# Counts of the experts held in registers, TensorE's branches in another order, and earlier signals in a mixture-of-experts layer

## The reference

```
logits = t @ w_router + b_router
top_val, top_idx = top_k(logits, 2);  gates = softmax(top_val)
for each expert e, with the tokens that chose it:
    y_e = (silu(x_e @ w_gate_e[e]) * (x_e @ w_up_e[e])) @ w_down_e[e]     # 1024 -> 3584 -> 1024
y = sum over a token's two experts of gate * y_e
```

## Time and profile before

| | |
|---|---|
| median of 3 runs | 1678.16 us (1676.92 to 1680.18) |
| the profiled execution | 1674.14 us, of which the span of its instructions is 1672.3 us |
| granted clock of TensorE, mean | 0.952 |
| TensorE busy | 1478.1 us, 88% of the span |
| DVE, ACT busy | 781.4 us, 589.6 us |
| read and written | 488.89 MB, 292 GB/s on average |

### The profile page before, as it was taken

One profiled execution on the slowest core, in us unless ns is written; L12 is line 12 of the kernel. 1 busy time (PEld: TensorE's weight loads), 2 busy tenths in 40 slices (PEclk: granted clock), 3 DMA queues, 4 the chain that ended last, 5 costly groups with the idle time before them and its releaser, 6 DMA issues.

```text
span 1672.3 us, 30627 instructions
## 1 busy us (share of the span) xinstructions
PE 1478.1 (88%) x12402; PEld 1185.7 (71%) x12403; DVE 781.4 (47%) x1097; ACT 589.6 (35%) x793; POOL 69.4 (4%) x66
## 2 busy tenths in 40 slices
PE   5999899999999998756579999999996679999894
PEld 3878778999977886644458875588985468888452
DVE  2584565565546655100028851177761036665112
ACT  2445253444344432100027740156551025554101
POOL 0010100000010111000000000000000000000002
PEclk8999999999999999987789999999998789999998
DMA  9644467745433528899999999997567996555893
GB/s 362 236 161 175 192 229 291 287 170 196 158 100 123 227 76 362 350 424 424 424 424 426 426 410 426 424 406 285 236 281 306 424 424 245 225 226 227 328 426 151
DMA packets 69183, 488.89 MB, mean 292 GB/s; under 512 B 7744, under 2 KB 7776, under 8 KB 11168
## 3 DMA queue, kind: packets, MB, share of 16 engines
q1 hardware_dynamic: 66800, 479.94, 71.0%
q10 hardware_dynamic: 1648, 4.59, 0.8%
q0 software_dynamic: 576, 2.10, 0.4%
HBM read 482.66 MB, written 3.93 MB: 291 GB/s over the span
## 4 chain that ended last, share of the span: by engine, by line
PE 44%; DMA 9%; issue 4%; DVE 2%; SPq 1%; ACT 1%; POOL 1%; ACTq 0%; POOLq 0%; DVEq 0%
PE PG L1443 9%; DMA ring<-in_experts 6%; PE PG L1500 4%; PE Y L1528 4%; PE Y L1455 4%; PE TRB L1500 4%; PE PG L1565 4%; DMA arena<-in_experts 3%; PE TRB L1506 3%; PE PG L1506 3%; PE Y L1613 2%; PE Y L1519 2%; PE TRB L1429 2%; SPq L786 1%; PE Y L1252 1%
## 5 line engine op out<-in xcount | busy, mean ns | idle before, releaser
L2570 DVE COPY arena<-TRB 128x64 f32<-128x64 f32 (+1 forms) x70 | 17.6, 251 | 343.0 <-PE TRB L1429 343.0
L1443 PE MATMUL PG<-ring,mixT 128*32 128x128 f32 (+1 forms) x1920 | 117.4, 352 | 65.2 <-issue 60.6
L1677 ACT ACTIVATE rope<-PG 64x128 f32<-64x128 f32 (+2 forms) x84 | 27.2, 324 | 378.7 <-PE PG L1443 356.2
L1443 PEld LDWEIGHTS PG<-ring,mixT 128*32 128x32 f32 (+1 forms) x1920 | 90.6, 139 | 95.9 <-issue 81.4
L1677 ACT ACTIVATE parts<-ring 128x2048 fp32r<-128x2048 f32 x81 | 151.8, 1901 | 9.1 <-DMA ring<-in_weights 4.0
L945 PE MATMUL PG<-h_parts,parts 128*128 128x512 f32 x432 | 152.9, 394 | 1.4 <-DVE arena L2448 1.4
L1443 PE MATMUL PG<-arena,mixT 128*32 128x128 f32 (+1 forms) x1664 | 102.2, 353 | 42.0 <-issue 42.0
L1443 PEld LDWEIGHTS PG<-arena,mixT 128*32 128x32 f32 (+1 forms) x1664 | 79.2, 140 | 69.4 <-issue 56.3
L947 PE MATMUL PG<-h_parts,parts 128*128 128x256 f32 x432 | 121.9, 282 | 0.0
L2433 DVE TENSOR_TENSOR parts<-ring,parts 128x2048 fp32r<-128x2048 f32 x42 | 95.1, 2289 | 30.4 <-ACT parts L1677 30.4
L2554 DVE TENSOR_TENSOR parts<-arena,parts 128x2048 fp32r<-128x2048 f32 x42 | 95.2, 2287 | 17.0 <-PE Y L1519 14.4
(11 more groups left out here) (384 smaller groups left out, 2839.8 us busy)
## 6 DMA issues: line engine op xcount, KB each, us to landing
ring<-in_experts SPq DMA_DIRECT2D x168, 1024.0 KB, 17.1
arena<-in_experts SPq DMA_DIRECT2D x168, 1024.0 KB, 18.9
ring<-in_weights SPq DMA_DIRECT2D x116, 1024.0 KB, 6.4
ring<-in_weights SPq DMA_DIRECT2D x4, 512.0 KB, 5.1
ypairs<-hT ACTq DMA_DIRECT2D x3, 512.0 KB, 7.0
tok<-in_x SPq DMA_DIRECT2D x1, 1024.0 KB, 9.0
result<-scr SPq DMA_DIRECT2D x2, 512.0 KB, 2.6
ring<-in_weights SPq DMA_DIRECT2D x2, 432.0 KB, 6.2
```

What stands on the lines that cost most here:

```text
L1443: last = mm(bank[i * n:(i + 1) * n, 0:width], xe[:, k, 0:n], w[k // 4][:, k % 4, i * width:(i + 1) * width], start=(k == 0), stop=(k == KD ...
L1677: return nc.scalar.activation(out_, in_, func, **kw)
```

## The change

- **Counts.** Each engine loads all eight counts into eight registers ahead of the loop, and shifts them down by one register (seven moves) with each expert. `pick` is gone.
- **Branches.** On TensorE `first_variant` is 32: its tests are 256, 192, 160, 128, 64, and the 32-row body comes right behind them, then 64, 128, 160, 192, 256. ACT and DVE keep 128.
- **First rows.** POOL copies the first expert's rows ahead of its loop, slices 0 to 5 and then 6 and 7, each when its slices are there; `xs_ready` becomes `xs_even` and `xs_odd`, and all gathers must be over (`xg_full`). The loop copies the other seven.
- **First halves.** A signal `gu_half` is raised when the first half of a stage's gate and up is multiplied. SyncE waits for it, instead of `gu_full`, before it refills the slot of that half. DVE waits for it, instead of `hi_used`, before the low part of the first half of the rows.

```diff
@@ experts()
-            rows = eng.alloc_register(label("rows"))
+            to_come = [eng.alloc_register(label(f"rows_{i}")) for i in range(NE)]
+            rows = to_come[0]
+            for i in range(NE):
+                eng.reg_load(to_come[i], cnt[0:1, i:i + 1])
             eng.reg_mov(turn, 0)
-            eng.br(label("pick"))
+            eng.br(label("tree"))
             with nc.body(label("next"), valid_engines=own):
                 eng.reg_add(turn, turn, 1)
-                eng.br_lt(turn, NE, on_true=label("pick"), on_false=label("done"))
-            with nc.body(label("pick"), valid_engines=own):
-                e = eng.snap(turn, min_val=0, max_val=NE - 1)
-                eng.reg_load(rows, cnt[0:1, bass.ds(e, 1)])
-                eng.br(label("tree"))
+                for i in range(NE - 1):
+                    eng.reg_mov(to_come[i], to_come[i + 1])
+                eng.br_lt(turn, NE, on_true=label("tree"), on_false=label("done"))
@@ last_use()
-                kind, s = expert_list[(i - SLOTS_E) % USES][0:2]
+                kind, s, *half = expert_list[(i - SLOTS_E) % USES]
+                if half == [0]:
+                    return gu_half, e * STAGES + ((STAGES if i >= SLOTS_E else 0) + s + 1)
                 return down_done if kind == "down" else gu_full, e * FT + ((FT if i >= SLOTS_E else 0) + 2 * s + 2)
@@ TensorE
+            pe.sem_inc(gu_half, STAGES)
...
@@ expert_whole, gate_up()
+                        if k == KD // 2 - 1:
+                            last.then_inc(gu_half, 1)
                     last.then_inc(gu_full, 2)
@@ expert_wide, gate_up_whole()
-                                used = last
-                        (used if h else last).then_inc(hi_used, 1)
-                    last.then_inc(gu_full, 2)
+                                last.then_inc(hi_used, 1)
+                        last.then_inc(gu_full if h else gu_half, 2 if h else 1)
@@ expert_wide, gate_up_half()
-                    if h == 1:
-                        last.then_inc(gu_full, 2)
+                    last.then_inc(gu_full if h else gu_half, 2 if h else 1)
@@ expert_split, gate_up_first()
-                        (before if h else last).then_inc(hi_used, 1)
+                        before.then_inc(hi_used, 1)
+                        if h == 0:
+                            last.then_inc(gu_half, 1)
@@ TensorE
-            experts(pe, "pe", expert)
+            experts(pe, "pe", expert, first_variant=32)
@@ POOL
-            po.wait_ge(xs_ready, KD)
+            po.wait_ge(xg_full, KD)
+            rows = xs[:, 0:KD * PAIRS].rearrange("p (k s) -> p k s", k=KD)
+            for a, b in ((0, KD - 2), (KD - 2, KD)):
+                po.wait_ge(xs_even, b // 2)
+                po.wait_ge(xs_odd, b // 2)
+                last = G.tensor_copy(xe[:, a:b, :], rows[:, a:b, 0:T])
+            last.then_inc(xe_ready, 1)
             po.wait_ge(table_ready, 1)
-            with po.Fori(0, NE) as e:
-                start = po.value_load(first[0:1, bass.ds(e, 1)], min_val=0, max_val=PAIRS)
-                po.wait_ge(gu_full, e * FT + FT)
+            with po.Fori(0, NE - 1) as e:
+                start = po.value_load(first[0:1, bass.ds(e + 1, 1)], min_val=0, max_val=PAIRS)
+                po.wait_ge(gu_full, e * FT + 2 * FT)
```

More of the change, by code:

```diff
@@ L589, in build @@
         xg_full = sem("xg_full")
-        xs_ready = sem("xs_ready")
+        xs_even, xs_odd = sem("xs_even"), sem("xs_odd")
+        gu_half = sem("gu_half")
         pad_zero = sem("pad_zero")
@@ L1603, in gate_up_half @@
                     lo_ready(e, q)
-                    gate_up_part(s, h, x_hi, w_lo_e[q % SLOTS_E], closes=(h == 1))
+                    last = gate_up_part(s, h, x_hi, w_lo_e[q % SLOTS_E], closes=(h == 1))
+                    if h == 0:
+                        last.then_inc(gu_half, 1)
                 def down_part(s, a, w, opens=False, closes=False):
@@ L1927, in _ @@
                 ae.wait_ge(xg_full, k + 1)
-                run(xs[:, k * PAIRS:(k + 1) * PAIRS], xg_banks[k], ACT.Copy).then_inc(xs_ready, 1)
+                run(xs[:, k * PAIRS:(k + 1) * PAIRS], xg_banks[k], ACT.Copy).then_inc(xs_even, 1)
             for b in range(TB):
@@ L1931, in _ @@
             ae.wait_ge(table_ready, 1)
-            ae.wait_ge(xs_ready, KD)
+            ae.wait_ge(xs_even, KD // 2)
+            ae.wait_ge(xs_odd, KD // 2)
             def silu(e, n, u, m):
@@ L2541, in _ @@
                 ve.wait_ge(xg_full, k + 1)
-                V.tensor_copy(xs[:, k * PAIRS:(k + 1) * PAIRS], xg_banks[k]).then_inc(xs_ready, 1)
+                V.tensor_copy(xs[:, k * PAIRS:(k + 1) * PAIRS], xg_banks[k]).then_inc(xs_odd, 1)
             def gated(e, n, u, m):
@@ L2621, in expert_wide @@
                     if s == 0:
-                        ve.wait_ge(hi_used, e * USES + 1)
+                        ve.wait_ge(gu_half, e * STAGES + (STAGES + 1))
                         low_rows_of(0)
```

## The result

The changed kernel takes 1689.49 us (median of 5 runs, 1687.18 to 1694.13), the kernel before 1680.18 (5 runs): ratio 1.0055, 95% interval 1.0036 to 1.0074. It is slower by 9 us; the prediction had 1673.7, in 1666 to 1685. The two profiled executions stand further apart, spans of 1687.7 and 1672.3 us: the one before lay 4.0 under the median of the runs shown with it, the one after on its own. So some 6 of the 15.4 us followed here are spread between executions.

The account below looks back on a forecast made before the run. DMA was taken to bound the first, second and sixth experts, TensorE's own start the third to fifth and from the seventh. Terms -6.3 +2.5 -0.7 +0.0 = -4.5 us gave 1673.7 us, range 1666 to 1685.

Parts of the forecast that it names:

- First rows and own signal: At the first expert: rows ready 2.1 us earlier and first block returned 1.85 earlier, together 3.95 us earlier DMA.
- Branch into the third expert: The free fall into 128 rows becomes a jump of 6.1 to 6.6 us; third expert starts 4.6 later.
- The fifth expert: Its start on TensorE: only 0.5 us later, after the fourth expert's waits for DMA absorb 4.1.
- cheap jumps into the fourth and fifth: TensorE's jumps into 64 rows after 128 (0.362 us) and 160 after 64 (0.467) would stay cheap.
- 4.1 to lose: In the fourth expert: waits for DMA worth 4.1 us that a later start could use up.
- Start of the sixth expert: Closing branch 2.8 us less, fall-through instead of jump 2.1 less, half signal 1.9 less; -6.3 in all with the fifth's +0.5.
- Seventh: Start of the seventh expert: closing branch +2.5 us, tests and step -0.7, making -4.5 in all.
- the free fall: Rival at the fall into the 32-row body: no load paid, total -11, 1667 us; chance 0.17.
- The border within the tests: Rival: last three tests behind a load border, two loads per branch to 128, 160, 64 rows; 1688.7 us; chance 0.14.
- the two cheap branches: Rival: jumps 128 to 64 and 64 to 160 rows become dear; second alone 1679.1 us, both 1684; chance 0.17.
- the change doesn't do what it says: Rival: first rows' gain eaten in third expert, fifth's closing branch stays 3.9, fall costs as the jump; 1678.6; chance 0.10.

Follow-up runs that it names:

- a3: The kernel before plus first rows in two pieces and the own signal for first halves, without counts in registers or the new body order: 1676.30 us, ratio 0.9976.
- a1: The changed kernel with only the order of TensorE's tests and bodies put back to the old one: 1675.42 us, ratio to the kernel before 0.9967.
- b2: The changed kernel with TensorE's 128-row body moved to the end, so the 160-row body follows the 64-row body: 1684.99 us, ratio to the kernel before 1.0045.
- b3: The changed kernel, its own order of bodies, with 78 signal instructions ahead in TensorE's program: 1681.65 us, ratio to the kernel before 1.0028.
- d2: The kernel before with a never-executed gap of 140 instructions ahead of TensorE's looped code: 1689.70 us, ratio to the kernel before 1.0071.
- d1: The kernel before with a never-executed gap of 60 instructions ahead of TensorE's looped code: 1672.79 us, ratio to the kernel before 0.9971.
- b1: The changed kernel with TensorE's 128-row body last and 84 signal instructions at the start of its program: 1674.82 us, ratio to the kernel before 0.9968.

## Why the prediction was wrong

By where each expert starts on TensorE, after against before (from the earlier trace rows and the branches above; for the sixth the last block's landing, 1354.86 against 1346.03):

```
start of       forecast   measured   the step's miss
third          +4.6       +7.5       2.9
fourth         +4.6       +8.1       0.6
fifth          +0.5       +14.7      10.7
sixth          -6.3       +8.8       0.9
seventh        -4.5       +14.4      3.8
eighth, end    -4.5       +15.4      1.0
```

*First rows and own signal:* right, 2.1 and 1.85 us forecast, 4.15 measured at the first block, and by the ratios 4.0 us of time in a3 and 5.5 in a1.

*Branch into the third expert:* right in kind. The closing branch was to go from 1.526 to 4.5 and went to 5.674, the jump was to cost 6.1 and took 6.5, and of the 3.95 only 2.5 were there when the closing branch began: −2.5 +4.1 +6.5 −0.6 = +7.5. The missing 1.5 are TensorE's own. Its last unit of gate and up in the second expert, in the kernel before and in the changed one:

```profile
858.19 1.95 PE L1443 MATMUL PG<-arena,mixT 128*32 128x128 f32 x64 [2.56 <-issue]
...
854.83 3.45 PE L1449 MATMUL PG<-arena,mixT 128*32 128x128 f32 x64 [2.37 <-issue]
```

It starts 3.4 us earlier, but takes 1.5 longer, since it runs at the lower of TensorE's two clock levels (1.2 GHz; granted clock 0.50 from 856 to 858 us), where it ran at the higher (2.4 GHz; 1.00 from 858 to 860). Ahead of it TensorE had stood for about as long in both, 2.4 and 2.6 us.

*The fifth expert is the step that failed*, "cheap jumps into the fourth and fifth" and "4.1 to lose". The rival was named, at 5.4 us and a chance of 0.17 with the other, but for a reason that the runs don't bear out here: the jump from 64 to 160 rows had been cheap not by few loads in between, but because the 160-row body began where the 64-row body ended, and the change put the 128-row body between them. That was readable from the order of the bodies. It cost 6.4. The closing branch behind 64 rows (0.42 to 3.97, 3.55) stood in no term, though the change moves that body's last piece as it moves the 32-row body's, from 152 to 44. And the fourth expert, from its start to its closing branch 83.5 us instead of 86.2, gave back 2.7, not 4.1. With 0.7 less for load and tests this makes the 10.7. b2 shows the first (0.368 with the old neighbour back), b3 the second: with a last piece of 122 and the same cheap entry (0.380) its closing branch took 0.419.

```profile
L702 PEldq COMPARE_BRANCH  x1: 419/419/419, 1072.3 to 1072.3; - x1
```

*Start of the sixth expert:* nearly right, −5.9 from fifth to sixth against −6.8. But by other terms: the closing branch gave 0.6 instead of 2.8 (last piece 21, not 41), the jump all of its 5.8, and 2.83 came back as the stop.

*Seventh:* the closing branch was to cost 2.5 more and cost 5.6: the 32-row body's last piece is 29 instructions and not 52. My lengths of bodies were counted from the trace's records and were short (1,117 for the 128-row body, which has 1,137).

*Rivals:* the free fall is refuted by the 2.83. The border within the tests didn't come: the seven moves are one instruction of 158 ns. It named nearly the time that was measured, 1688.7, but that is luck, since its mechanism is absent. Of the two cheap branches one became dear, the second, for which the prediction had 1679.1. Of the rival in which the change doesn't do what it says, two of three terms are there: the gain at the first rows was gone by the third expert, and the fifth's closing branch stayed at 3.3; but the fall cost 2.83 and not as much as the jump.

## What to carry to other kernels

Where an engine's program is larger than its store of code and branches by data, lay out its bodies first: list for each branch how many instructions stand behind the last border ahead of it, who its neighbour is, and how many pieces are loaded between two uses, for any edit in front moves all of these. A gap that isn't executed moves them without other work; here 60 instructions gave 0.3% and 140 took 0.7%. Then read the branches' records, for the count of the last piece alone didn't foretell all of them. When one engine's branch becomes cheap, look at once at the same branch on the engines that it exchanges data with.

## What the runs showed of the hardware that I had not expected

- A load of code on TensorE costs 4.2 to 7.1 us where nothing covers it, and where the same instructions stand was worth 12 us up (d2) and 5 down (d1) of 1680.
- A last piece of 21 to 29 instructions of a 32-row body hid nothing of the closing branch's load (5.4 to 6.1 us), 135 and more all but 0.3 to 1.5. Behind a 64-row body that had been entered by a dear jump, 36 to 44 instructions were enough (0.20 to 0.21).
- By a count of the code, a piece was still held after eight later loads and gone after nine.
- Signals at a program's start aren't free on an idle engine: 78, 84, 106 and 140 put the first matmul at 13.1, 14.0, 17.3 and 22.4 us, from 10.8. With 60 it came at 11.2, as it did with a gap of 140 and no signals.
- ScalarE pays for its own jump at the sixth expert, 2.4 us in the kernel before and 5.5 in b1, unseen as long as TensorE pays as much.
